# Prompt attention logits as three fp32r passes over split queries and keys

## The reference, cut to what matters

```python
def sparse_attention(q, qi, wi, q_chunk, k_all, v_all, ki_all, k_chunk, top_k):
    ...
    _, idx = lax.top_k(score, top_k)
    ...
    logits = jnp.einsum('bqgrd,bqkgd->bqgrk', qg, k_sel, preferred_element_type=jnp.float32) * ATTN_SCALE
    logits = jnp.where(valid[:, :, None, None, :], logits, -jnp.inf)
    p = jax.nn.softmax(logits, axis=-1)
    o = jnp.einsum('bqgrk,bqkgd->bqgrd', p.astype(v_sel.dtype), v_sel)
```

## Time and profile before

| | us |
|---|---|
| time, median of 3 runs | 1388.13 (1387.41 to 1389.83) |
| the profiled execution's own time | 1387.29 |
| its span, first to last instruction | 1385.3 |
| PE busy | 1285.4 (93%) |
| DVE busy | 828.8 (60%) |
| POOL busy | 473.5 (34%) |
| ACT busy | 403.7 (29%) |

### The profile page before, as it was taken

One profiled execution on the slowest core, in us unless ns is written; L12 is line 12 of the kernel. 1 busy time (PEld: TensorE's weight loads), 2 busy tenths in 40 slices (PEclk: granted clock), 3 DMA queues, 4 the chain that ended last, 5 costly groups with the idle time before them and its releaser, 6 DMA issues.

```text
span 1385.3 us, 20882 instructions
## 1 busy us (share of the span) xinstructions
PE 1285.4 (93%) x7577; PEld 1093.4 (79%) x7577; DVE 828.8 (60%) x2059; ACT 403.7 (29%) x908; POOL 473.5 (34%) x769
## 2 busy tenths in 40 slices
PE   5999999999989999998999999999999989999940
PEld 5978999999979999995555555899788758888830
DVE  4554778888999988816666556242565622222237
ACT  5554222122121122224555434100332212222112
POOL 4800595878872126540000000220011232323324
PEclk9999999999999999999999899999999989999975
DMA  7201232222213231002000221744201168999856
GB/s 249 70 24 42 75 82 78 38 74 56 61 57 112 65 97 48 1 21 76 1 16 1 64 65 32 285 148 173 109 32 46 39 233 306 386 342 339 302 217 268
DMA packets 71116, 163.75 MB, mean 118 GB/s; under 512 B 12529, under 2 KB 38721, under 8 KB 69873
## 3 DMA queue, kind: packets, MB, share of 16 engines
q1 hardware_dynamic: 56929, 129.31, 26.7%
q0 software_dynamic: 12656, 27.62, 6.0%
q10 hardware_dynamic: 1440, 5.58, 1.0%
HBM read 137.81 MB, written 39.21 MB: 128 GB/s over the span
## 4 chain that ended last, share of the span: by engine, by line
PE 88%; POOL 4%; DVE 4%; ACT 2%; DMA 1%; issue 1%; POOLq 0%; SPq 0%; ACTq 0%; DVEq 0%
PE bank L765 11%; PE bank L766 11%; PE bank L767 11%; PE bank L1123 8%; PE bank L952 5%; PE bank L916 4%; PE bank L1129 4%; PE bank L939 3%; PE bank L1023 3%; PE bank L1017 2%; PE bank L887 2%; PE bank L1035 2%; PE bank L1034 2%; PE bank L1036 2%; PE bank L1116 2%; PE bank L977 2%
## 5 line engine op out<-in xcount | busy, mean ns | idle before, releaser
L1583 DVE MAX8 small<-region_kv 128x8 f32<-128x272 f32 (+4 forms) x241 | 190.2, 828 | 51.3 <-DVE region_kv L1588 51.2
L765 PE MATMUL bank<-h_hi,w_hi 128*128 128x384 f32 (+1 forms) x576 | 196.1, 340 | 0.0
L766 PE MATMUL bank<-h_lo,w_hi 128*128 128x384 f32 (+1 forms) x576 | 196.0, 340 | 0.0
L1588 DVE MATCH_REPLACE8 region_kv<-small,region_kv 128x272 f32<-128x272 f32 (+4 forms) x241 | 195.5, 818 | 0.0
L767 PE MATMUL bank<-h_hi,w_lo 128*128 128x384 f32 (+1 forms) x576 | 194.4, 338 | 0.0
L1867 POOL TENSOR_TENSOR w_lo<-w_stage,w_hi 128x512 fp32r<-128x512 f32 x64 | 80.8, 1297 | 149.5 <-ACT w_hi L1197 149.4
L765 PE MATMUL bank<-w_hi,h_hi 128*128 128x256 f32 x448 | 129.9, 290 | 1.4 <-ACT region_q L1257 1.4
L767 PE MATMUL bank<-w_hi,h_lo 128*128 128x256 f32 x448 | 125.9, 281 | 0.0
L766 PE MATMUL bank<-w_lo,h_hi 128*128 128x256 f32 x448 | 125.9, 281 | 0.0
L767 PEld LDWEIGHTS bank<-h_hi,w_lo 128*128 128x128 f32 x576 | 108.7, 189 | 0.0
L766 PEld LDWEIGHTS bank<-h_lo,w_hi 128*128 128x128 f32 x576 | 108.2, 188 | 0.6
(11 more groups left out here) (260 smaller groups left out, 2771.4 us busy)
## 6 DMA issues: line engine op xcount, KB each, us to landing
w_stage<-in_w_in SPq DMA_DIRECT2D x72, 256.0 KB, 3.3
region_kv<-in_xa SPq DMA_DIRECT2D x16, 512.0 KB, 5.6
region_q<-in_wg SPq DMA_DIRECT2D x12, 512.0 KB, 9.0
region_q<-in_wu SPq DMA_DIRECT2D x12, 512.0 KB, 20.0
region_q<-in_wd SPq DMA_DIRECT2D x12, 512.0 KB, 22.8
region_h<-in_wg SPq DMA_DIRECT2D x12, 512.0 KB, 11.0
region_h<-in_wu SPq DMA_DIRECT2D x12, 512.0 KB, 20.0
region_h<-in_wd SPq DMA_DIRECT2D x12, 512.0 KB, 23.2
```

The lines of the kernel that those rows point to most:

```text
L765: mm(out, st_hi(k), mv_hi(k), start=(k == 0), stop=False)
L766: mm(out, st_hi(k), mv_lo(k), start=False, stop=False)
L1583: nc.vector.max(m8[:, q, :], x).then_inc(dve_c, 1)
L1588: nc.vector.match_replace(x, m8[:, q, :], x, TAKEN).then_inc(dve_c, 1)
```

## The change

The logits of the prompt's groups are made in three fp32r passes instead of one float32 product: high query * high key, rest query * high key, high query * rest key. The logits of the samples are not changed.

- **Keys** are split once, at the start of the stage: ACT casts `kT` to `k_hi` in six pieces, DVE subtracts for key head 0 and POOL for key head 1, into `k_lo`, which lies over `kT`.
- **Queries** are split for one group at a time: ACT's `q_upper(PG[st + 2])` after the exponentials and copies of step st, DVE's `q_rest(PG[st + 2])` after `oevac(PG[st])`. The high part goes to one of two buffers `q_hi`, the rest to the part of `o_hi` that the group's output will take later. The first two groups are split ahead of the loop or in step -1.
- **Probabilities**: `PT` has 3 buffers instead of 4, and `PB` and `PT` start 1520 elements later, which makes room for the query and key parts.
- **Chunks** have an even width: 348, 348 and 344 columns for block 7 instead of 347, 347 and 346. All others were even.

```diff
+        KEY_CHUNKS = splits(SAMPLE0)
+        def q_at(x):
+            n = PG.index(x)
+            return q_hi[n % 2], (slice(REP * x[2], REP * x[2] + REP), slice(x[1] * P, (x[1] + 1) * P)), n
...
@@ PE, qk @@
-                    last = mm(b[:, 0:c1 - c0], qT[:, REP * g + r, i * P:(i + 1) * P], kT[:, g, c0:c1],
-                              start=True, stop=True)
+                    qh, (_, ts_), nq = q_at(x)
+                    out, lo = b[:, 0:c1 - c0], o_hi[:, REP * g + r, ts_]
+                    if r == 0 and m == 0:
+                        pe.wait_ge(q_high, nq + 1)
+                    if nq < KVH and r == 0:
+                        pe.wait_ge(k_high, 3 * nq + m + 1)
+                    mm(out, qh[:, r, :], k_hi[:, g, c0:c1], start=True, stop=False)
+                    if r == 0 and m == 0:
+                        pe.wait_ge(q_low, nq + 1)
+                    mm(out, lo, k_hi[:, g, c0:c1], start=False, stop=False)
+                    if nq < KVH and r == 0:
+                        pe.wait_ge(k_low if nq == 0 else k_low1, m + 1)
+                    last = mm(out, qh[:, r, :], k_lo[:, g, c0:c1], start=False, stop=True)
...
@@ ACT @@
+            def q_upper(x):
+                qh, (hs, ts_), n = q_at(x)
+                if n >= 2:
+                    act.wait_ge(a_s, S_AT[PG[n - 2]] + REP * len(chunks_of(PG[n - 2])))
+                cp(qh[:, :, :], qT[:, hs, ts_]).then_inc(q_high, 1)
...
+            q_upper(PG[0])
+            for g in range(KVH):
+                for c0, c1 in KEY_CHUNKS:
+                    cp(k_hi[:, g, c0:c1], kT[:, g, c0:c1]).then_inc(k_high, 1)
+            q_upper(PG[1])
...
                     expo(PG[st + 1], r)
+                if st >= 0 and st + 2 < NPG:
+                    q_upper(PG[st + 2])
...
@@ DVE @@
+            def q_rest(x):
+                qh, (hs, ts_), n = q_at(x)
+                dve.wait_ge(q_high, n + 1)
+                tt(o_hi[:, hs, ts_], qT[:, hs, ts_], qh[:, :, :].bitcast(F32), ALU.subtract).then_inc(q_low, 1)
+            q_rest(PG[0])
+            for m, (c0, c1) in enumerate(KEY_CHUNKS):
+                dve.wait_ge(k_high, m + 1)
+                tt(k_lo[:, 0, c0:c1], kT[:, 0, c0:c1], k_hi[:, 0, c0:c1].bitcast(F32), ALU.subtract).then_inc(k_low, 1)
...
                 if st >= 0:
                     oevac(PG[st])
+                if -1 <= st < NPG - 2:
+                    q_rest(PG[st + 2])
                 if st - 1 in S_STEP:
                     oevac(S_STEP[st - 1])
...
@@ POOL @@
+            for m, (c0, c1) in enumerate(KEY_CHUNKS):
+                pool.wait_ge(k_high, 3 + m + 1)
+                tt(k_lo[:, 1, c0:c1], kT[:, 1, c0:c1], k_hi[:, 1, c0:c1].bitcast(F32), ALU.subtract).then_inc(k_low1, 1)
             for b in range(3):
                 new_keys(b)
```

More of the change, by code:

```diff
@@ L72, in splits @@
     k = -(-n // most)
-    w = -(-n // k)
+    w = -(-n // (2 * k)) * 2
     return [(c, min(c + w, n)) for c in range(0, n, w)]
@@ L104, in build @@
                 wao_lo[q] = ao_weights.enter_context(nc.sbuf_tensor(f"wao_lo{q}", [P, KD, P], F32R))
+        with ExitStack() as key_rest:
+            key_rest.enter_context(nc.sbuf_tensor("values_first", [P, 2560], F32))
+            k_lo = key_rest.enter_context(nc.sbuf_tensor("keys_lo", [P, KVH, COLS], F32R))
         RK = sb("region_kv", [P, 10240])
@@ L127, in build @@
             stage_t = sb_early("w_stage", [P, 4 * 512], F32)
+        with ExitStack() as query_parts:
+            query_parts.enter_context(nc.sbuf_tensor("sample_first", [P, 7760], F32))
+            k_hi = query_parts.enter_context(nc.sbuf_tensor("keys_hi", [P, KVH, SAMPLE0], F32R))
+            q_hi = [query_parts.enter_context(nc.sbuf_tensor(f"queries_hi{q}", [P, REP, P], F32R)) for q in range(2)]
         RH = sb("region_h", [P, 9344])
@@ L250, in build @@
         zs = nflat[:, 1024:1520].rearrange("p (a b c) -> p a b c", a=2, b=DEC_B)
-        PB = [view(RT, 0, REP, 1040), view(RT, 4160, REP, 1040)]
-        PT = view(RT, 8320, 4, 512)
+        PB = [view(RT, 1520, REP, 1040), view(RT, 5680, REP, 1040)]
+        PT = view(RT, 9840, 3, 512)
         PBS = [nbuf_t[:, 0:SK], nbuf_t[:, SK:2 * SK]]
@@ L512, in build @@
         zero_ready = sem("zero_ready")
+        q_high = sem("queries_high")
+        q_low = sem("queries_rest")
+        k_high = sem("keys_high")
+        k_low = sem("keys_rest")
+        k_low1 = sem("second_keys_rest")
         a_s = sem("logits_done")
@@ L951, in p_values @@
                 rows = META if j == 0 else P
-                last = mm(bank[5 + slot_of(x)][:, :], vS[0:rows, j, g * HD:(g + 1) * HD], PT[0:rows, t % 4, :],
+                last = mm(bank[5 + slot_of(x)][:, :], vS[0:rows, j, g * HD:(g + 1) * HD], PT[0:rows, t % 3, :],
                           start=(j == 0), stop=(j == nb - 1))
@@ L975, in s_values @@
                         rows = P if j < 4 else 32
-                        src = PT[0:rows, t % 4, j * P:(j + 1) * P] if j < 4 else PT[0:rows, (t + 1) % 4, 0:P]
+                        src = PT[0:rows, t % 3, j * P:(j + 1) * P] if j < 4 else PT[0:rows, (t + 1) % 3, 0:P]
                         last = mm(ob[:, 64 * gg:64 * gg + 64], v[0:rows, j, gg * HD:(gg + 1) * HD],
@@ L1374, in tevac @@
                     rows = META if j == 0 else P
-                    cp(PT[0:rows, t % 4, :], bank[3 + t % 2][0:rows, :]).then_inc(a_te, 1)
+                    cp(PT[0:rows, t % 3, :], bank[3 + t % 2][0:rows, :]).then_inc(a_te, 1)
                 elif j == 0:
-                    cp(PT[:, t % 4, :], bank[3 + t % 2][:, :]).then_inc(a_te, 1)
+                    cp(PT[:, t % 3, :], bank[3 + t % 2][:, :]).then_inc(a_te, 1)
                 else:
-                    cp(PT[0:32, t % 4, 0:P], bank[3 + t % 2][0:32, 0:P]).then_inc(a_te, 1)
+                    cp(PT[0:32, t % 3, 0:P], bank[3 + t % 2][0:32, 0:P]).then_inc(a_te, 1)
             def wao_upper(c):
```

4 lines of the change are left out of this document (added).

## The result

The changed kernel takes 1389.17 us (median of 12 runs, 1387.72 to 1394.51), the kernel before 1387.52 us (median of 12 beside it, 1385.47 to 1389.83). The ratio is 1.002, with a 95% interval of 1.0011 to 1.003: about 3 us slower, where 5 us faster was forecast. The profiled execution took 1388.47 us, with a span of 1386.3.

What follows compares the result with a forecast made beforehand. PE was taken to bound most of the stage, except the start and some late waits. Gains of -6.7 us and +1.5 for the start gave -5.2: 1387.3 to 1382.1, forecast 1382.9 us, 8-in-10 range 1379.0 to 1387.0.

Steps and rivals of the forecast that it cites:

- start: Up to the end of step -1: splitting queries and keys delays ttr and exponential, 1.4 to 1.6 us later, taken as +1.5.
- step 0: First full step, with no oevac ahead of it: gains the full 1.25 us from cheaper passes.
- steps 1 to 6: Full steps: gains after waits of 1.0 us each in 1 and 2, 0.65 in 3 and 4, 0.3 in 5 and 6.
- step 7: Begins with a sample's ttr, which q_rest pushes back: 0.25 us gained of 0.63.
- step 8: q_rest falls into DVE's wait for the sample's values, so the step gains its full 0.63 us.
- steps 10 to 14: Steps 10 to 12 gain 0.15 us each; steps 13 and 14 were put at 0.05 us each, entering the sum as +0.1.
- q_rest in the loop: DVE's added 0.61 us ahead of ttr makes PE's fourth call of a step wait 0.1 to 0.5 us.
- The rate of the passes: Logits calls: three passes cost 1.38 ns per column against 1.68, 0.63 us per 456-column call, 11.4 us gained in all.
- The late steps: From step 9 PE is partly held by copies behind exponentials, so only part of the cheaper passes' gain arrives.
- half-clock stretches move: Samples' steps: stretches cost 1.7 us each; two more give 1386.3 us (0.19), two fewer 1379.5 (within a shared 0.20).
- passes do not run at the projection's rate: Logits calls: a gap of 0.1 us per call over 100 calls loses 10 us, about 1389 us; chance 0.08.
- the clock falls in the full steps: Steps 1 to 6: new waits bring a half-clock stretch each, 10.2 us in all, 1393.1 us; chance 0.05.

Runs made afterwards that it cites:

- e8: The changed kernel plus 42 matmuls that nobody reads, placed in PE's waits: 1382.67 us, ratio 0.9962 to the kernel before.
- e7: The kernel before plus 42 matmuls that nobody reads, placed in PE's waits: 1375.7 us, ratio 0.9928 to the kernel before.
- e9: e1 plus the same unread matmuls in PE's waits: 1369.55 us, ratio 0.9873 to the kernel before.
- e1: The changed kernel with q_rest ahead of oevac on DVE, nothing else: 1382.07 us, ratio 0.9959 to the kernel before.
- after_again: The changed kernel run again without any edit: 1390.11 us, ratio 1.0026 to the kernel before.
- before_again: The kernel before run again without any edit: 1387.37 us, ratio 1.0004.
- e6: e4 plus unread matmuls in PE's waits (12 before step 0, 3 per sample step, 6 before the output projection): 1368.19 us, ratio 0.9879 to the kernel before.
- e4: e1 plus the rest-query pass made last and key casts moved from ACT to DVE and POOL: 1381.61 us, ratio 0.9952 to the kernel before.

## Why the prediction was wrong, point by point

The working added up to -5.2 us. The same sum with what the kernels with fills measured (e8 less e7; e9 less e7 in steps 8 to 14, where e8 has two half-clock stretches and e9 none). Their clock is held in these steps; in the start e8 has one half-clock stretch and e7 none, so that term holds some clock too:

| term | predicted | measured |
|---|---|---|
| start | +1.5 | +2.45 |
| step 0 | -1.25 | -1.18 |
| steps 1 to 6 | -3.9 | **+4.70** |
| step 7 | -0.25 | +0.15 |
| step 8 | -0.63 | -0.58 |
| step 9 | -0.35 | -0.48 |
| steps 10 to 14 | -0.35 | -0.27 |
| sum | -5.2 | +4.8 |

Of the 10.0 us between forecast and measured sum, 8.6 lie in one term.

- **The step that failed is "q_rest in the loop".** It counted what stands behind `q_rest` on DVE, found `ttr`, and asked when PE would next want a bank from `ttr`: at the fourth call, "a wait of 0.1 us" to 0.5. It never asked who reads what `q_rest` itself writes. That is PE's second pass of the step's first call, which PE wants 0.65 us (four transposes and a high pass) after the step begins, while `q_rest` can end at 2.2 us at the earliest: `oevac` cannot start before PE's last values. The text even had that number (first `ttr` at +2.15). 2.2 less 0.65 is the stall of 1.5 us, six times over, 8.9 us in e8's list. From the start of the first pass to that of the second it is 1.92 us in the changed kernel's step 1 and 0.29 in e1's, 1.63 more, or 9.8 us for six steps out of the 10.6. With `q_rest` ahead of `oevac` the same steps are 5.85 us shorter than before (e9 less e7), which is about the 5.6 us that the working has for them before it takes off waits. In the late steps DVE's order is the same, but e8's list has no such stall there, and in steps 10 to 12, at full clock in both, e8 and e9 take the same time (40.18 and 40.17 us): there the term held.
- **The rate of the passes** was right. In the changed kernel's timeline above a call of 456 columns takes 656.14 - 655.52 = 0.62 us, against 0.63 forecast and 0.765 before. Step 0, where no stall lies, gives -1.18 us with the clock held and -1.30 in the profiles of after and before, each with 3.4 us at half clock there; after_again has twice that and gives only -0.42 against before_again. The rival of passes with gaps (0.1 us a call) is refuted. The measured 0.62 us against 0.765 also confirms that three passes are not three quarters of four.
- **The start** costs 2.45 to 2.5 us instead of 1.5, in all five profiles of the changed kernel and of e1, with and without fills. The first `ttr` comes 3.11 us after the last query copy in after_again, against 1.46 in before: 1.65 later, against 1.4 forecast. The other 0.8 us lies between that `ttr` and the scaling of head 0 (4.59 us against 3.79 in before_again), and there the clock is at half: the passes of 348 columns are 0.29 us apart. Three of them take longer than the `ttr` behind them, so DVE waits for PE ahead of the second and the third chunk of the second head, 0.34 and 0.33 us, which it did not before. The stretch at half clock comes after a new wait of PE for the split keys, 1.64 us; that the wait brings it about is likely and not shown. The timeline of PE and DVE in after_again:

```profile
621.11 0.40 PE L940 MATMUL bank<-keys_hi,queries_hi 128*128 128x348 f32 x1 [1.64 <-ACT keys_hi L1427]
...
624.22 0.49 PE L940 MATMUL bank<-keys_hi,queries_hi 128*128 128x348 f32 x1
624.51 0.49 PE L943 MATMUL bank<-keys_hi,o_hi 128*128 128x348 f32 x1
```

```profile
624.46 0.52 DVE L1670 CUSTOM_DVE_ANT_0 region_t<-bank,region_kv 128x348 f32<-128x348 f32 x1
...
625.33 0.52 DVE L1670 CUSTOM_DVE_ANT_0 region_t<-bank,region_kv 128x348 f32<-128x348 f32 x1 [0.34 <-PE bank L946]
626.19 0.52 DVE L1670 CUSTOM_DVE_ANT_0 region_t<-bank,region_kv 128x344 f32<-128x344 f32 x1 [0.33 <-PE bank L946]
```

- **Step 7** gained nothing with `q_rest` late (+0.15) and 0.47 with it early (e9). The working allowed 0.38 of its 0.63 us for the sample's delayed `ttr`; between e8 and e9 the place of `q_rest` is worth 0.62 us there.
- **The late steps** were right: with the clock held, steps 10 to 14 take 61.04 us in e7 and 60.77 in e9. Cheaper passes are worth almost nothing there.
- **The rival "half-clock stretches move"** did happen, but it was booked as one or two stretches of 1.7 us around the sum. It is the larger size: e7 against before shows 10 us that the kernel before loses to it, twice what the change was meant to bring. The stretches between 617 and 880 us came to 24 and 31 us in two profiles of before, 27 and 35 of after (37 with the end of the last one, at 882.5 us). So the change did not clearly lose or win by them.
- **The rival "passes do not run at the projection's rate"** has an error in its sum: 10 us on top of 1382.9 are 1392.9, not "about 1389".
- **The rival "the clock falls in the full steps"**, the one that ended slower, had the right sign and the wrong mechanism. After the first half-clock stretch of step 0 the profile of the changed kernel has none until 767 us; six stalls of 1.5 us in steps of 15 to 19 us did not bring the clock down. With the same stalls e8 has 0.99 over all 15 steps. The Trainium skill, "TensorE: Matmul & The Clock Gate", section "A second HAM failure mode: psum-queue depth-cycling", describes a clock that swings where PE idles briefly between groups of matmuls; the stalls of these steps did not set that off.

What stays open: the work sums to +4.8 us, e8 against e7 gives 1.4 to 8, which holds it, and the plain kernels give 1.5 to 4.2 (1.0011 to 1.003). In the profiles the difference lies ahead of the stage, where the two kernels do the same work. From the last query copy to step 15 the changed kernel takes 4.8 us longer in the first pair of profiles and 3.8 in the second, but it reaches that copy 3.9 and 2.1 us earlier: near 400 us both profiles of before have some 7 us at half clock, those of the changed kernel none and 3.4. Whether that is chance or follows from the change, two profiles of each do not show.

## What to carry to other kernels

When an instruction is put into an engine's queue, ask two questions and not one: who waits for what stands behind it, and who reads what it writes, and when; the second was worth 10 us here and was cured by exchanging two lines, so that the new instruction lies in a wait that its engine already has. Before judging an edit of a few us on a kernel whose clock moves, read the granted clock of each stretch, and compare the steps at 1.00 only. Filling PE's waits with matmuls that nobody reads was worth more than the change itself; e6 and e9 beat the kernel before by 1.2 and 1.3%.

## What the runs showed of the hardware

- Within one kernel, time mostly follows the mean granted clock of the run. The six runs of e8 go from 1384.34 us at 0.971 to 1378.71 at 0.975, those of e7 from 1383.62 at 0.968 to 1373.22 at 0.977: 14 and 12 us for 0.01. It is no law: one run of the kernel before has 1395.48 us at 0.92, where almost all its others have 1381 to 1390 us at 0.963 to 0.968.
- Work that nobody reads can shorten a kernel. In e7, 42 matmuls of 512 bf16 columns, 12 + 8 * 3 + 6, brought 10 us. They run in waits of PE; the twelve ahead of step 0, of which the trace records eleven, take 2.54 us there and leave 1.49 us of a wait that was 4.08 (timeline of PE in e7):

```profile
628.21 2.54 PE L959 MATMUL bank<-cbf 128*128 128x512 bf16 x11
632.24 0.60 PE L939 MATMUL bank<-consts,region_t 128*16 128x128 f32 x4 [1.49 <-DVE region_t L1648]
```

- A fall can outlast full load. In e1 the output projection's passes follow each other without a gap from 866.5 us on, at 0.32 us each (1.2 GHz, the clock at half), and only from 872.7 at 0.175 (2.4 GHz), 6 us later. PE's timeline of e1:

```profile
866.98 0.52 PE L1048 MATMUL bank<-o_lo_prompt,wao_hi 128*128 128x384 f32 x1
867.30 0.52 PE L1052 MATMUL bank<-o_hi,wao_lo 128*128 128x384 f32 x1
...
872.70 0.34 PE L1048 MATMUL bank<-o_lo_prompt,wao_hi 128*128 128x384 f32 x1
872.87 0.34 PE L1052 MATMUL bank<-o_hi,wao_lo 128*128 128x384 f32 x1
```

- POOL's operations can take longer beside DVE's. Those that rotate the last queries took 0.34 to 0.52 us each while DVE split keys (e4), and 0.25 us each without that (e9).
- A half-clock stretch costs about half its length. Step 0 of the kernel before has 3.4 us at half clock and loses 1.68 (20.76 against 19.08 in e7); its steps 7 to 14 have 17.0 us and lose 7.3 (117.68 against 110.36), somewhat less than half, since PE waits there for DVE and ACT as well.
